# Gated linear attention: statistics interleaved with the output tiles, and the router's constants moved to sliding attention

## The reference

```python
    o = o_intra + jnp.einsum('bhncd,bhndv->bhncv', q_dec, states)
    ...
    o = rmsnorm(o, g_head) * jax.nn.silu(r.astype(jnp.float32)).reshape(B, L, GLA_HEADS, GLA_DV)
    return o.reshape(B, L, GLA_V).astype(hn.dtype) @ w_out
```

## Time and profile before

| what | us |
|---|---|
| median of 3 runs (1813.57 to 1815.26) | 1815.05 |
| the profiled execution | 1812.95 |
| its span | 1811.1 |
| PE busy | 1753.5 (97%) |
| DVE busy | 1079.1 (60%) |
| ACT busy | 705.7 (39%) |
| mean granted TensorE clock | 0.988 |

### The profile page before, as it was taken

One profiled execution on the slowest core, in us unless ns is written; L12 is line 12 of the kernel. 1 busy time (PEld: TensorE's weight loads), 2 busy tenths in 40 slices (PEclk: granted clock), 3 DMA queues, 4 the chain that ended last, 5 costly groups with the idle time before them and its releaser, 6 DMA issues.

```text
span 1811.1 us, 31911 instructions
## 1 busy us (share of the span) xinstructions
PE 1753.5 (97%) x12556; PEld 1420.2 (78%) x12556; DVE 1079.1 (60%) x1923; ACT 705.7 (39%) x1119; POOL 21.2 (1%) x26
## 2 busy tenths in 40 slices
PE   9999999999999999998999999997999999999996
PEld 8999989889999999997899999997963333333332
DVE  6775565687765877669787656868772222222223
ACT  5444553363444544445644446955331011110110
POOL 0000000000000000000000001000010000000000
PEclk9999999999999999999999999998999999999998
DMA  6545334344554355541245545442769999999996
GB/s 234 184 165 203 121 132 149 36 163 162 184 188 162 119 185 185 198 149 71 94 162 185 217 167 187 151 155 102 316 245 396 428 428 427 427 427 428 428 428 257
DMA packets 42339, 409.71 MB, mean 226 GB/s; under 512 B 5304, under 2 KB 5304, under 8 KB 7056
## 3 DMA queue, kind: packets, MB, share of 16 engines
q1 hardware_dynamic: 40032, 402.21, 57.1%
q0 software_dynamic: 1936, 5.79, 1.6%
q10 hardware_dynamic: 288, 0.52, 0.1%
HBM read 405.87 MB, written 2.63 MB: 226 GB/s over the span
## 4 chain that ended last, share of the span: by engine, by line
PE 82%; DVE 11%; DMA 4%; ACT 1%; issue 1%; DVEq 0%; SPq 0%; ACTq 0%
PE ps L598 81%; DMA soon<-w_gate_up 4%; PE ps L602 2%; DVE w_lo L1635 1%; DVE h L1741 1%; DVE x_lo L1697 1%; DVE h L1745 1%; DVE rs L1677 1%; DVE arena L1999 1%; DMA raw<-w_units 1%; DVE arena L2027 0%; DVE small L2005 0%; DVE arena L1919 0%; DVE small L2004 0%; DVE arena L2147 0%
## 5 line engine op out<-in xcount | busy, mean ns | idle before, releaser
L598 PE MATMUL ps<-x_hi,w_hi 128*128 128x256 f32 (+1 forms) x2144 | 619.3, 289 | 12.9 <-DVE x_lo L1695 4.5
L598 PE MATMUL ps<-x_lo,w_hi 128*128 128x256 f32 (+1 forms) x2144 | 612.9, 286 | 0.0
L598 PE MATMUL ps<-x_hi,w_lo 128*128 128x256 f32 (+1 forms) x2144 | 611.2, 285 | 0.0
L1635 DVE TENSOR_TENSOR w_lo<-raw,w_hi 128x1024 fp32r<-128x1024 f32 (+1 forms) x352 | 441.0, 1291 | 77.6 <-ACT w_hi L1245 77.1
L598 PEld LDWEIGHTS ps<-x_hi,w_hi 128*128 128x128 f32 x2144 | 406.2, 189 | 24.1 <-issue 9.4
L1245 ACT ACTIVATE w_hi<-raw 128x1024 fp32r<-128x1024 f32 (+1 forms) x352 | 379.6, 1111 | 110.3 <-PE ps L598 84.9
L598 PEld LDWEIGHTS ps<-x_hi,w_lo 128*128 128x128 f32 x2144 | 408.1, 190 | 0.0
L598 PEld LDWEIGHTS ps<-x_lo,w_hi 128*128 128x128 f32 x2144 | 407.3, 190 | 0.2
L598 PE MATMUL ps<-hid_hi,w_hi 128*128 128x272 f32 (+1 forms) x720 | 206.0, 286 | 0.7 <-DVE hid_lo L1697 0.3
L598 PE MATMUL ps<-hid_hi,w_lo 128*128 128x272 f32 (+1 forms) x720 | 204.6, 284 | 0.0
L598 PE MATMUL ps<-hid_lo,w_hi 128*128 128x272 f32 (+1 forms) x720 | 204.0, 283 | 0.0
(11 more groups left out here) (328 smaller groups left out, 1964.2 us busy)
## 6 DMA issues: line engine op xcount, KB each, us to landing
raw<-w_units SPq DMA_DIRECT2D x144, 1024.0 KB, 4.8
soon<-w_gate_up SPq DMA_DIRECT2D x34, 2048.0 KB, 18.2
late<-w_gate_up SPq DMA_DIRECT2D x30, 2048.0 KB, 18.6
raw<-w_out_units SPq DMA_DIRECT2D x32, 1408.0 KB, 6.0
soon<-w_down SPq DMA_DIRECT2D x16, 2048.0 KB, 18.9
late<-w_down SPq DMA_DIRECT2D x16, 2048.0 KB, 18.5
bias_rows<-kT POOLq DMA_DIRECT2D x1, 1536.0 KB, 33.4
cst<-table SPq DMA_DIRECT2D x1, 1448.0 KB, 11.7
```

The lines of the kernel that those rows point to most:

```text
L598: return nc.tensor.matmul(out_ap, lhsT, rhs, start=start, stop=stop, skip_group_check=True)
L1635: v.tensor_tensor(part(w_lo, c, 0, n), raw_slot(u, j * n, n), part(w_hi, c, 0, n).bitcast(F32), ALU.subtract).then_inc(lo_made, 1)
```

## The change

- PE makes the sum of squares of head `i - 1` between the two output tiles of head `i`, and that of the last head behind its tiles. The output tiles take banks 4 to 7 twice instead of 0 to 7 once.
- ACT takes the root of each head straight from PSUM, with the scale and EPS in the instruction (`head_root`), in the order tiles 0 to 3, root 0, tiles 4 and 5, root 1, tiles 6 and 7, root 2, high parts 0 to 3, root 3, high parts 4 to 7. The table for Sqrt is loaded ahead of the first tile. DVE's four L1912 are gone.
- DVE's order is written out anew: gate product, reciprocal and scaling by head, and the low parts behind them.
- The router's constants leave their place before `gout`. PE makes them in sliding attention after the scores of groups 0 and 1, into bank 6; DVE copies them after the maxima of group 1.

```diff
--- before.py
+++ after.py
@@ -374,9 +374,8 @@
         tiles("att", [0, 1, 2, 3], 4)
         tiles("kwT", [4, 5, 6, 7], 4)
         tiles("kv", list(range(8)), 12)
-        tiles("o", list(range(8)), 8)
+        tiles("o", [4, 5, 6, 7], 8)
         tiles("gst", MAIN, 4)
-        tiles("rconst", [5], 1)
         plan["gout"] = (units.take(4), Tiles(uses, MAIN, 8))
         tiles("stat3", [7], 1)
         tiles("stat4", [7], 1)
@@ -391,6 +390,7 @@
         tiles("stat8", [7], 1)
         plan["sq"] = (units.take(4), Tiles(uses, MAIN, 8))
         tiles("qrot", [4, 5], 8)
+        tiles("rconst", [6], 1)
         tiles("ss", MAIN, 16)
         tiles("sT", [4, 5, 6], 24)
         tiles("sv", [7], 8)
@@ -817,34 +817,36 @@
                 bank = free(T.at(3 * i + 2))
                 mm(bank[:, 0:256], kw[0:64, 128:256], v1[0:64, :], True, True).then_inc(full[T.at(3 * i + 2)[0]], 1)
 
-            for i in range(GH):
-                taken(plan["att"].at(i))
-                taken(plan["kv"].at(3 * i + 2))
-                for half in range(2):
-                    t = plan["o"].at(2 * i + half)
-                    bank = free(t)
-                    c0 = i * GDV + half * P
-                    mm(bank[:, 0:P], g_v[:, c0:c0 + P], g_att[:, i * TA:i * TA + P], True, False)
-                    mm(bank[:, P:2 * P], g_v[:, D + c0:D + c0 + P], g_att[:, i * TA + P:i * TA + 2 * P], False, False)
-                    mm(bank[:, SEQ:TA], g_vm[0:META, c0:c0 + P], g_att[0:META, i * TA + SEQ:(i + 1) * TA], False, False)
-                    for c in range(4):
-                        st = g_s[:, (i * 4 + c) * GDV + half * P:(i * 4 + c) * GDV + (half + 1) * P]
-                        m = mm(bank[:, c * CH:(c + 1) * CH], st, g_q[:, i * TA + c * CH:i * TA + (c + 1) * CH],
-                               False, c == 3)
-                    m.then_inc(full[t[0]], 1)
-            for i in range(GH):
+            def head_tile(i, half):
+
+                t = plan["o"].at(2 * i + half)
+                bank = free(t)
+                c0 = i * GDV + half * P
+                mm(bank[:, 0:P], g_v[:, c0:c0 + P], g_att[:, i * TA:i * TA + P], True, False)
+                mm(bank[:, P:2 * P], g_v[:, D + c0:D + c0 + P], g_att[:, i * TA + P:i * TA + 2 * P], False, False)
+                mm(bank[:, SEQ:TA], g_vm[0:META, c0:c0 + P], g_att[0:META, i * TA + SEQ:(i + 1) * TA], False, False)
+                for c in range(4):
+                    st = g_s[:, (i * 4 + c) * GDV + half * P:(i * 4 + c) * GDV + (half + 1) * P]
+                    m = mm(bank[:, c * CH:(c + 1) * CH], st, g_q[:, i * TA + c * CH:i * TA + (c + 1) * CH],
+                           False, c == 3)
+                m.then_inc(full[t[0]], 1)
+
+            def head_squares(i):
+
                 taken(plan["o"].at(2 * i + 1))
                 t = plan["gst"].at(i)
                 bank = free(t)
                 mm(bank[:, 0:TA], C("ones"), tile(g_sq, 2 * i, TA), True, False)
                 mm(bank[:, 0:TA], C("ones"), tile(g_sq, 2 * i + 1, TA), False, True).then_inc(full[t[0]], 1)
-            t = plan["rconst"].at(0)
-            bank = free(t)
-            for i, name in enumerate(("ln1_g", "ln1_b")):
-                for k in range(KT):
-                    m = mm(bank[:, i * 64:i * 64 + 36], W(name, k, k + 1).to_broadcast([P, P]),
-                           W("w_route", k * 36, (k + 1) * 36), k == 0, k == KT - 1)
-            m.then_inc(full[t[0]], 1)
+
+            for i in range(GH):
+                taken(plan["att"].at(i))
+                taken(plan["kv"].at(3 * i + 2))
+                head_tile(i, 0)
+                if i:
+                    head_squares(i - 1)
+                head_tile(i, 1)
+            head_squares(GH - 1)
             u0, T = plan["gout"]
             for j in range(4):
                 project(u0 + j, T, 2 * j, X, TA, x_base=None if j else 16,
@@ -916,7 +918,7 @@
                 def outputs(g):
                     t = V.at(g)
                     bank = free(t)
-                    if g == 0 and values is not None:
+                    if g == 0 and names[0] == "bs":
                         taken(plan["mv"][1].at(3))
                     taken(TT.at(len(turns) * (g + 1) - 1))
                     for n in range(2):
@@ -939,11 +941,21 @@
                         outputs(g - 1)
                 outputs(groups - 1)
 
+            def router_constants():
+
+                t = plan["rconst"].at(0)
+                bank = free(t)
+                for i, name in enumerate(("ln1_g", "ln1_b")):
+                    for k in range(KT):
+                        m = mm(bank[:, i * 64:i * 64 + 36], W(name, k, k + 1).to_broadcast([P, P]),
+                               W("w_route", k * 36, (k + 1) * 36), k == 0, k == KT - 1)
+                m.then_inc(full[t[0]], 1)
+
             attend(("ss", "sT", "sv"), 8, 0, a_p, a_pT, P + META, SWA_ROW,
                    lambda g, hs, n: s_q[hs, g * SEQ + n * P:g * SEQ + (n + 1) * P],
                    lambda g, hs, key, size: kT[hs, g // 4, key:key + size],
                    lambda g, b, key, size: vs[0:size, key // P, (2 * (g // 4) + b) * 64:(2 * (g // 4) + b) * 64 + 64],
-                   SWA_SEGS, SWA_TURNS, lambda g: pe.wait_ge(q_roped, g + 1))
+                   SWA_SEGS, SWA_TURNS, lambda g: pe.wait_ge(q_roped, g + 1), router_constants)
             u0, T = plan["sout"]
             for j in range(4):
                 project(u0 + j, T, 2 * j, X, SEQ, x_base=None if j else 56,
@@ -1398,15 +1410,23 @@
                 nc.scalar.activation(g_kwT[:, i * 384:i * 384 + 256], bank[:, 0:256], ACT.Copy)
                 nc.scalar.activation(g_kwT[0:META, i * 384 + 256:(i + 1) * 384], bank[0:META, 256:384], ACT.Copy)\
                     .then_inc(evac[t[0]], 1)
+            def head_root(t, dst, n, of, eps):
+
+                nc.scalar.activation(dst, filled(t)[:, 0:n], ACT.Sqrt, bias=small[:, eps:eps + 1], scale=1.0 / of)\
+                    .then_inc(evac[t[0]], 1)
+
+            nc.scalar.preload_act_table(ACT.Sqrt)
             for i in range(8):
                 t = plan["o"].at(i)
                 bank = filled(t)
                 nc.scalar.activation(tile(g_sq, i, TA), bank[:, 0:TA], ACT.Square)
                 nc.scalar.activation(tile(g_o, i, TA), bank[:, 0:TA], ACT.Copy, scale=W("gla_norm", i % 2, i % 2 + 1))\
                     .then_inc(evac[t[0]], 1)
-            for i in range(GH):
-                root(plan["gst"].at(i), tile(g_kw, i, TA), tile(g_kw, i, TA))
+                if i % 2 and i > 1:
+                    head_root(plan["gst"].at(i // 2 - 1), tile(g_kw, i // 2 - 1, TA), TA, GDV, 264)
             for i in range(8):
+                if i == 4:
+                    head_root(plan["gst"].at(3), tile(g_kw, 3, TA), TA, GDV, 264)
                 act.wait_ge(scaled, i + 1)
                 high(i, tile(g_o, i, TA), TA)
             branch_out("gout", 3, 3, par, TA)
@@ -1903,31 +1923,40 @@
                 mine(tb)
                 v.scalar_tensor_tensor(state(3), state(2), decay(2), filled(tc)[:, 0:256], ALU.mult, ALU.add)\
                     .then_inc(evac[tc[0]], 1)
-            for i in range(8):
-                o = tile(g_o, i, TA)
-                mine(plan["o"].at(i))
-                did(v.tensor_tensor(o, o, tile(g_r, i, TA), ALU.mult))
-            for i in range(GH):
-                t = plan["gst"].at(i)
-                v.tensor_scalar(tile(g_kw, i, TA), filled(t)[:, 0:TA], 1.0 / GDV, EPS, ALU.mult, ALU.add)\
-                    .then_inc(evac[t[0]], 1)
-            own()
-            for i in range(GH):
+            def gate_head(i):
+
+                for o_i in (2 * i, 2 * i + 1):
+                    o = tile(g_o, o_i, TA)
+                    mine(plan["o"].at(o_i))
+                    did(v.tensor_tensor(o, o, tile(g_r, o_i, TA), ALU.mult))
+
+            def scale_head(i):
+
                 r = tile(g_kw, i, TA)
-                stds[0] += 1
-                dve.wait_ge(std_made, stds[0])
+                mine(plan["gst"].at(i))
                 then(v.reciprocal(r, r))
                 for half in range(2):
                     o = tile(g_o, 2 * i + half, TA)
                     v.tensor_tensor(o, o, r, ALU.mult).then_inc(scaled, 1)
-                    if i or half:
-                        low(2 * i + half - 1, TA, src=tile(g_o, 2 * i + half - 1, TA))
-            low(7, TA, src=tile(g_o, 7, TA))
+
+            def head_low(i):
+
+                for m in (2 * i, 2 * i + 1):
+                    low(m, TA, src=tile(g_o, m, TA))
+
+            gate_head(0)
+            gate_head(1)
+            scale_head(0)
+            gate_head(2)
+            scale_head(1)
+            gate_head(3)
+            head_low(0)
+            scale_head(2)
+            head_low(1)
+            scale_head(3)
+            head_low(2)
+            head_low(3)
             residual("gout", 3, TA, lambda m: gain(4, m))
-            t = plan["rconst"].at(0)
```

(14 more changed lines are left out.)

## The result

The changed kernel takes 1806.25 us (median of 5 runs, 1805.96 to 1807.04) against 1815.15 us (median of 5, 1813.57 to 1815.38): ratio 0.9946, 95% interval 0.9931 to 0.9960 (the ratio of the two medians by themselves is 0.9951). Forecast was 1809.6, with a range from 1807.8 up. So it is faster, as forecast, but by 8.9 us where 5.4 were worked out, and outside the range. The profiled execution took 1806.25 us too, its span 1804.4; before it was 1812.95 and 1811.1, so the two profiled executions are only 6.7 us apart. That the two differences disagree is the first hint.

The account below looks back on a forecast made before the run. PE bounds the kernel except where it waits for a DVE and ACT chain; 4.95 + 0.5 + 0 = 5.4 us took the profiled 1812.95 to 1807.5 and the median 1815.05 to 1809.6, range 1807.8 to 1813.3.

Parts of the forecast that it names:

- The path: Output tiles to projection: last tile, root, four heads on DVE, last operand; PE ended unit 0 at 360.36.
- PE's order: Three sums of squares between output tiles: last tile ends at 343.45, 2.2 us later; only the last sum waits.
- ACT: Two roots fit between tiles, table load moves ahead; high parts 1 to 3 and root 3 end about 346.5.
- DVE: Heads 0 and 1 finish during PE's tiles; low parts end at 353.25 instead of 359.22, 6.0 us earlier.
- the projection: Output projection, unit 0: starts at 345.75, ends at 355.4 instead of 360.36, gain 4.95 us, bounds 4.3 and 6.0.
- Start of the tiles: First output tile no longer waits for its bank and follows the last `kv` matmul: gain 0.5 us.
- End of the projection: Waits for a weight transfer and ACT's last square shrink: gain 0.5 us, bounds 0 and 1.0.
- The constants: Router's constants moved into sliding attention: up to 0.2 us lost there, at most 0.2 us back earlier, sum 0.
- The clock rival: Clock falls in the output projection around two PE waits: gain only 2.3 to 4.2 us, time 1811.9, chance 0.27.
- the stretch at 1294 to 1297: Evidence against the clock's fall: PE busy 1.15 of 3.00 us there, yet the clock stayed at 1.00.

Follow-up runs that it names:

- the second trace of before: The kernel before, run again unchanged against itself: 1816.65 us over 12 runs, ratio 1.0007.
- constants only: The kernel before with only the router's constants moved to sliding attention: 1817.04 us over 12 runs, ratio 1.0011.
- banks only: The kernel before with one edit, the output tiles taking banks 4 to 7 twice: 1812.2 us, one run.
- no interleave: The changed kernel with all eight output tiles first and the four heads' sums, roots and scaling behind them: 1810.02 us, one run.
- before filled: The kernel before plus unread matmuls, 2 ahead of the gate matmuls and 8 in sliding attention: 1810.73 us over 12 runs, ratio 0.9974.
- GLA only: The changed kernel with the router's constants back in front of the output projection: 1810.43 us over 10 runs, ratio 0.9964.
- the delays: The changed kernel with 4, 8 and 12 matmuls added in the third feed-forward part, far ahead of attention: 1809.62, 1810.12 and 1813.53 us.

## Why the prediction was wrong

**The path** was read rightly: last tile, root, DVE's heads, last operand. **PE's order, ACT, DVE, the projection**: the terms summed to 4.95 us, and 4.96 were measured in every trace. The expected waits of PE were 1.0 and twice 1.8 us, the measured ones 0.86, 1.46 and 1.53; the low parts end 8.8 us behind the last gate product, as worked out. **Start of the tiles**: 0.5, measured 0.49. **End of the projection**: 0.5, measured 0.55 (0.64 against the second trace of before); it was the middle of bounds of 0 and 1.0, so that it lay so near is in part luck. **The constants**: 0 with 0.2 us each way, measured -0.1 up to attention and +0.2 in it. The sum of 5.4 us is what was measured of the edit.

**What failed** is the step from there to the median: "so I let the gain go through to the end undiminished", and "it lay 2.1 us under the median of the runs", by which 1807.5 became 1809.6. The time of all that is not edited was taken as that of one trace, and the 2.1 us as a constant, without a reason for either. The gain does go through, but the time around it is not fixed. Of the 3.35 us between 1809.6 and 1806.25, the profiled executions show 1.25: the gate stage took 79.60 us where it had taken 81.07 (and the stretch ahead of it 0.14 more). The other 2.1 are the distance from profiled execution to median, which was 0 this time.

The range failed with it. Its low end, 1807.8, is the sum of the upper bounds of the edit's own terms, 6.0 + 1.0 + 0.2, and holds nothing for a spread. The three runs at hand were 1.7 us wide, 28 runs of one kernel 9.8 us. The granted clock falls in some executions and not in others, and sliding attention alone takes 41.35 to 49.9 us for it. In these 28, 1812.17 us goes with a mean clock of 0.989 and 1821.09 with 0.982. Chance has its share in the miss too: of the four medians of the changed kernel, 1806.25 and 1807.19 lie outside the range and 1808.74 and 1808.73 inside it.

**The clock rival** was asked in one place only, the projection, where it did not come: 1.00 in all three windows. It did not come in any of the 12 traces of kernels with the heads interleaved, while all 6 others (before, its repeat, constants only, banks only, no interleave, before filled) have about 6.8 us of low clock there. The reasons given against it were poor, though. The 36-column matmuls were blamed for the fall in the projection before; constants only fell without them, and GLA only kept 1.00 with them. And the stretch at 1294 to 1297, at 1.00 in the one trace that was read, is no evidence: behind the same wait the clock is low in 14 of the 18 traces, here in banks only:

```profile
1295.50:1298.90 3.40, 3.40 (x18) 3.40 (x17) 3.23 (x11) 0.87 (x1) 0.00 (x0) 0.50 1.05 441
```

The rule behind the rival, from the Trainium skill, "TensorE: Matmul & The Clock Gate", section "A second HAM failure mode: psum-queue depth-cycling", is a clock that swings between groups of matmuls with short idles. Attention is made of such groups, and a low clock does cost time there, 8.2 us between the two traces of before; but what those traces show is not a swing from group to group, it is one low stretch of 3.4 us in the first and one of 23.9 us in the second.

**Open**: 5.4 us are the edit's own, shown. The mean over 98 runs of before is 1816.2 us and over 31 runs of the changed kernel 1808.0, 8.2 us apart. Where the other 2.8 us come from is not shown. That it is granted clock is likely, since the mean clock of the runs goes with their time, but mean clocks don't prove it: 6.8 us of low clock in the projection are gone in every trace, which raises the mean without giving time. Nor is it only a few long runs: from the tenth percentile to the ninetieth the runs of the two kernels are 7.7 to 8.9 us apart, and the shortest of each 6.4. And no trace was taken of a typical run of the kernel before: its two are of 1812.95 and 1819.35 us. In them the stages that are not edited are not longer than in the changed kernel's (see the table), only attention in the second is. Whether the surplus comes from the shift in time or from something in the new order, the delays did not settle.

## What to carry to other kernels

Look for a chain in which one engine does all heads after the last one has arrived, and let it do each head when that head is there; price it by what is left behind the last arrival, not by the sum of the work moved. Work that fills a wait is free until the wait is gone, and here it was still free then, since the consumer had other waits behind (36.26 against 36.28 us with and without it). Before putting a range on a gain of a third of a per cent, profile the same kernel several times, list the stretches in which the granted clock is under 1.00 in any of the traces, and ask what the time is with and without each: one trace shows neither all of them nor how long they last. And compare two kernels by the stages between the same matmuls, which repeated to 0.1 us here where medians of the same pair differed by 2.4.

## What the hardware showed that was not expected

The low clock can last while PE is busy. In the second trace of before, PE was busy 22.54 of 23.90 us in one unbroken stretch at 0.50:

```profile
837.90:861.80 23.90, 22.54 (x146) 16.77 (x147) 16.28 (x56) 14.27 (x50) 0.00 (x0) 0.50 0.00 1
```

At full clock the stage has slack on PE (busy 37.93 of 41.35 us with 8 matmuls added), and DVE is busy 37.55 us. So a short fall costs little: of the six traces with a mean clock of 0.92 there, five take 41.56 to 41.74 us and one, banks only, 42.34. At 0.88 it takes 43.36 us, at 0.82 to 0.85 45.6 to 46.9, at 0.76 49.58.

```profile
825.03:868.39 43.36, 41.59 (x434) 32.04 (x433) 37.97 (x126) 28.52 (x103) 0.00 (x0) 0.88 0.01 2
```

```profile
828.32:874.69 46.37, 40.56 (x401) 30.11 (x400) 37.78 (x124) 28.64 (x103) 0.00 (x0) 0.82 0.01 2
```

Both traces with 8 added matmuls that compute nothing had 1.00 in this stage. But so had one with 2, and one with nothing added in it (12 matmuls far ahead), and two of the 12 runs with 8 took 1824 us; that the added matmuls hold the clock up is not shown.
